# Two transformer blocks on one core: the opening's half slabs shared out anew, four attention levels with late queries only, one joint reordered

## The reference

```python
def first_block(x, ...):                     # DEPTH = 2
    for i in range(2):
        h = rms_norm(x, g[0])
        m = neighborhood_attention(h) if i == 0 else diff_attention(h)
        x = x + rms_norm(m, g[1])
        f = conv_glu_ffn(rms_norm(x, g[2]))
        x = x + rms_norm(f, g[3])
        gate = sigmoid(rms_norm(x, g[4]) @ ple_w_gate[i])
        x = x + gate * (p[i] @ ple_w_proj[i])

def second_block(h, ...):
    h = h + 0.5 * swiglu(rms_norm(h))
    o_hg = hgrn2_chunkwise(hq, log_f, k, v)  # gated linear attention, 4 heads, decay per key channel
    o_mla = causal_block_attention(q, k, v)
    h = h + concat(o_hg, o_mla) @ w_out
    h = h + 0.5 * swiglu(rms_norm(h))
    h = h + sigmoid(rms_norm(h) @ w_ple_gate) * (p @ w_ple_proj)
    return rms_norm(h)
```

## Time and profile before

| what | value |
|---|---|
| median of 3 runs | 1193.83 us (1193.71 to 1195.09) |
| the profiled execution | 1193.79 us |
| its span, first to last instruction | 1191.9 us |
| granted TensorE clock, mean | 0.998 |
| PE, PEld busy | 99%, 86% |
| DVE, ACT, POOL busy | 78%, 56%, 12% |
| weights and inputs read | 213.60 MB, 180 GB/s over the span |

### The profile page before, as it was taken

The page is one execution under the profiler, slowest core; times in us unless marked ns, Lnnn a source line. Parts: engine busy times, 40 slices in busy tenths (PEclk is TensorE's granted clock), DMA queues, the critical chain, the costliest instruction groups (busy, mean ns, idle before and its releaser), DMA issues.

```text
span 1191.9 us, 17766 instructions
## 1 busy us (share of the span) xinstructions
PE 1179.1 (99%) x6915; PEld 1028.1 (86%) x6915; DVE 933.1 (78%) x1270; ACT 665.0 (56%) x1059; POOL 139.0 (12%) x265
## 2 busy tenths in 40 slices
PE   8999999999999999999999999999999999999997
PEld 7998988888889989888888988888898888888886
DVE  6866898898777689989888898766776878766765
ACT  6756644444867786544446745444586664444445
POOL 5300600000300011000003100000206410000002
PEclk9999999999999999999999999999999999999999
DMA  9758376655544345665555575556455147556540
GB/s 297 223 156 269 124 244 207 210 179 178 190 139 148 129 163 195 212 205 185 182 173 179 184 230 189 189 187 203 136 191 177 44 161 228 176 197 204 185 142 36
DMA packets 151671, 215.83 MB, mean 181 GB/s; under 512 B 7002, under 2 KB 116956, under 8 KB 151588
## 3 DMA queue, kind: packets, MB, share of 16 engines
q1 hardware_dynamic: 148124, 207.46, 53.1%
q0 software_dynamic: 1760, 3.94, 1.3%
q10 hardware_dynamic: 1704, 3.28, 0.9%
HBM read 213.60 MB, written 1.06 MB: 180 GB/s over the span
## 4 chain that ended last, share of the span: by engine, by line
PE 93%; DVE 3%; ACT 1%; DMA 1%; issue 1%; POOL 0%; SPq 0%; POOLq 0%; ACTq 0%; DVEq 0%
PE work L2491 25%; PE work L2494 13%; PE acc L2072 10%; PE acc L2073 10%; PE acc L2074 10%; PE work L2072 5%; PE work L2073 5%; PE work L2074 5%; PE work L2094 1%; PE work L2480 1%; PE work L2468 1%; DVE w_lo L1357 1%; PE work L2482 1%; PE work L2619 1%; PE acc L2129 1%; PE acc L2270 1%
## 5 line engine op out<-in xcount | busy, mean ns | idle before, releaser
L1357 DVE TENSOR_TENSOR w_lo<-raw,w_hi 128x2048 fp32r<-128x2048 f32 (+1 forms) x192 | 436.0, 2277 | 51.5 <-ACT w_hi L752 51.5
L752 ACT ACTIVATE w_hi<-raw 128x2048 fp32r<-128x2048 f32 (+1 forms) x192 | 363.5, 1899 | 69.0 <-PE work L2494 59.4
L2491 PE MATMUL work<-hT_both,w_hi 128*128 128x512 f32 x1280 | 318.8, 391 | 0.0
L2491 PEld LDWEIGHTS work<-hT_both,w_hi 128*128 128x128 f32 x1280 | 234.8, 188 | 45.1
L2494 PEld LDWEIGHTS work<-hT_both,w_lo 128*128 128x128 f32 x1280 | 174.6, 190 | 12.5
L2494 PE MATMUL work<-hT_both,w_lo 128*128 128x256 f32 x1280 | 178.5, 282 | 0.0
L2072 PE MATMUL acc<-w_hi,aux_hi 128*128 128x512 f32 x400 | 158.0, 395 | 0.0
L2073 PE MATMUL acc<-w_lo,aux_hi 128*128 128x512 f32 x400 | 156.7, 392 | 0.0
L2074 PE MATMUL acc<-w_hi,aux_lo 128*128 128x512 f32 x400 | 155.8, 390 | 0.0
L1131 ACT ACTIVATE aux_hi<-Z 128x256 fp32r<-128x256 f32 x88 | 36.9, 419 | 195.4 <-DVE Z L1780 107.4
L1751 DVE TENSOR_REDUCE Z<-work 128x256 f32<-128x512 f32 x88 | 60.6, 689 | 89.5 <-PE work L2494 87.8
(11 more groups left out here) (283 smaller groups left out, 1740.2 us busy)
## 6 DMA issues: line engine op xcount, KB each, us to landing
raw<-in_ffn_w_in SPq DMA_DIRECT2D x44, 1024.0 KB, 5.1
raw<-in_ffn_w_out SPq DMA_DIRECT2D x22, 1024.0 KB, 5.1
raw<-in_w_gate SPq DMA_DIRECT2D x22, 1024.0 KB, 5.3
raw<-in_w_up SPq DMA_DIRECT2D x22, 1024.0 KB, 5.3
raw<-in_w_down SPq DMA_DIRECT2D x22, 1024.0 KB, 4.9
raw<-in_da_w_qkv SPq DMA_DIRECT2D x12, 1024.0 KB, 5.3
raw<-in_na_w_qkv SPq DMA_DIRECT2D x10, 1024.0 KB, 7.3
raw<-in_ple_w_gate SPq DMA_DIRECT2D x8, 1024.0 KB, 5.2
```

The lines of the kernel that those rows point to most:

```text
L752: act.activation(w_hi[:, n % RING, 0:size], raw[:, n % RAW, 0:size], ACT.Copy).then_inc(hi_done, 1)
L1357: dve.tensor_tensor(w_lo[:, n % RING, 0:size], raw[:, n % RAW, 0:size], w_hi[:, n % RING, 0:size].bitcast(F32), ALU.subtract).then_inc(lo_ ...
L2491: pe.matmul(b.rearrange("p (e s) -> p e s", e=2), v[0][:, k, cols(c % 2)], hT_both[:, k, :, :], start=k == 0, stop=False)
```

## The change

There are three parts.

1. **Opening.** ACT casts half 2 in place of half 3, ahead of the last four blocks of tile 0. POOL casts half 1, makes the second tile's root, casts half 3 and makes its low part too; DVE loses that low part. PE and SP wait on the semaphores that now belong to each half.
2. **Levels.** On levels 1 to 4 PE's moving operand is the late queries alone, 64 in place of 128, read as runs of r; the result lies packed in 64 columns for each head and tile. DVE's masked copy reads and writes 256 elements in place of 512. Level 0 and level 5 stay.
3. **Joint.** ACT and DVE take `feed(b + 6)` ahead of the sums of squares and of the scaling of tile 0; DVE adds pieces 2 and 3 before the blocks of tile 0, and piece 4 in their middle; ACT does the squares of tile 1 in three places. PE turns tile 0 in the middle of the last gate piece, behind that piece's wait, and turns tile 1 before the last step of tile 0's value rows.

```diff
@@ -370,6 +370,7 @@
         half_landed = [sem(f"half_landed{i}") for i in range(2 * FIRST)]
         act_half_hi, pool_half_hi, half_lo = sem("act_half_hi"), sem("pool_half_hi"), sem("half_lo")
+        pool_half_lo = sem("pool_half_lo")
         hi_done, lo_done = sem("hi_done"), sem("lo_done")
@@ -570,6 +571,8 @@
                 if n >= RAW:
                     sp.wait_ge(lo_done, n - RAW + 1)
+                    if n == RAW + 1:
+                        sp.wait_ge(pool_half_lo, 1)
                 if n == RELOAD:
@@ -630,10 +633,14 @@
             late_rows(pool)
             powers("pre0.0")
-            for i in (1, 2):
-                pool.wait_ge(half_landed[i], 16)
-                pool.tensor_copy(weight_half(w_hi, i), weight_half(raw, i)).then_inc(pool_half_hi, 1)
+            pool.wait_ge(half_landed[1], 16)
+            pool.tensor_copy(weight_half(w_hi, 1), weight_half(raw, 1)).then_inc(pool_half_hi, 1)
             powers("pre0.1")
+            pool.wait_ge(half_landed[3], 16)
+            pool.tensor_copy(weight_half(w_hi, 3), weight_half(raw, 3)).then_inc(pool_half_hi, 1)
+            pool.wait_ge(pool_half_hi, 2)
+            pool.tensor_tensor(weight_half(w_lo, 3), weight_half(raw, 3), weight_half(w_hi, 3).bitcast(F32),
+                               ALU.subtract).then_inc(pool_half_lo, 1)
             for i in range(32):
@@ -844,16 +851,18 @@
                 if ph == 2:
                     gates(2, 1)
+                    feed(b + 6)
                     pre(3, 0)
-                    feed(b + 6)
                     gates(2, 2)
                     gates(2, 3)
-                    tile_parts(3, 0, range(4))
+                    tile_parts(3, 0, range(2))
+                    pre(3, 1, (0,))
+                    tile_parts(3, 0, range(2, 4))
+                    pre(3, 1, (1,))
                     gates(2, 4)
                     tile_parts(3, 0, range(4, 6))
-                    pre(3, 1, (0, 1))
+                    pre(3, 1, (2,))
                     tile_parts(3, 0, range(6, 8))
-                    pre(3, 1, (2,))
                     feed(b + 7)
@@ -1293,8 +1302,8 @@
             tile_parts(0, 0, range(4))
             pre(0, 1, (1,))
+            high_half(2)
             tile_parts(0, 0, range(4, 8))
-            high_half(3)
             act.dma_start(z(11864, 12120), bass.AP(w["da_lambda"].tensor, 0, [[0, P], [1, 256]])).then_inc(lam_loaded, 16)
@@ -1494,14 +1503,13 @@
                     add_gated(2, 0)
                     add_gated(2, 1)
+                    feed(b + 6)
                     normed(3, 0)
-                    feed(b + 6)
-                    tile_parts(3, 0, range(4))
                     add_gated(2, 2)
                     add_gated(2, 3)
-                    tile_parts(3, 0, range(4, 6))
+                    tile_parts(3, 0, range(4))
                     add_gated(2, 4)
-                    tile_parts(3, 0, range(6, 8))
+                    tile_parts(3, 0, range(4, 8))
                     normed(3, 1)
@@ -1878,9 +1886,19 @@
                             continue
                         evacuated(dve, G[f"lev{i - 1}"] + q)
-                        m = lmask[:, i, :]
-                        dve.copy_predicated(A[:, 4 * q:4 * q + 4, :], bass.AP(m.tensor, m.offset, [m.ap[0], [0, 4], [1, P]]),
-                                            bank(g, 4)).then_inc(bank_free[g % WORK], 1)
+                        if i == QUAD:
+                            m = lmask[:, i, :]
+                            dve.copy_predicated(A[:, 4 * q:4 * q + 4, :],
+                                                bass.AP(m.tensor, m.offset, [m.ap[0], [0, 4], [1, P]]),
+                                                bank(g, 4)).then_inc(bank_free[g % WORK], 1)
+                            continue
+                        n, r = P // (2 * LEVELS[i]), LEVELS[i]
+                        m = lmask[:, i, r:P]
+                        to = A[:, 4 * q:4 * q + 4, r:P]
+                        dve.copy_predicated(bass.AP(to.tensor, to.offset, [to.ap[0], [P, 4], [2 * r, n], [1, r]]),
+                                            bass.AP(m.tensor, m.offset, [m.ap[0], [0, 4], [2 * r, n], [1, r]]),
+                                            bank(g)[:, 0:S].rearrange("p (a b r) -> p a b r", a=4, b=n))\
+                            .then_inc(bank_free[g % WORK], 1)
 
@@ -1981,12 +1999,12 @@
 
             def low_half(i):
-                if i in (1, 2):
-                    dve.wait_ge(pool_half_hi, i)
+                if i == 1:
+                    dve.wait_ge(pool_half_hi, 1)
                 else:
-                    dve.wait_ge(act_half_hi, 1 + i // 3)
+                    dve.wait_ge(act_half_hi, 1 + i // 2)
                 dve.tensor_tensor(weight_half(w_lo, i), weight_half(raw, i), weight_half(w_hi, i).bitcast(F32),
-                                  ALU.subtract).then_inc(lo_done if i % 2 else half_lo, 1)
+                                  ALU.subtract).then_inc(lo_done if i else half_lo, 1)
 
@@ -2022,7 +2040,6 @@
             normed(0, 1)
             low_half(2)
-            low_half(3)
             tile_parts(0, 1)
@@ -2168,14 +2185,16 @@
                             ins.then_inc(used, 1)
 
-            def value_rows(ph, half, kh, t):
+            def value_rows(ph, half, kh, t, ks=range(4)):
                 v, g = slab(B[ph] + VALUE_SLABS[ph][half] + kh), G[f"v{ph}.{half}.{t}"]
                 b = open_bank(pe, g) if kh == 0 else work[:, g % WORK, :]
-                for k in range(4):
+                for k in ks:
                     if ph == 3 and half == 0:
                         split_done(pe, ph, t, 4 * kh + k)
                     ins = product3(b, both(hT, every, 4 * kh + k, cols(t)), both(v, every, k, every),
                                    kh == 0 and k == 0, kh == 1 and k == 3)
+                if ks[-1] < 3:
+                    return
                 if kh == 1:
@@ -2208,10 +2227,12 @@
                 for j in range(2):
                     if j == 1:
-                        if ph + 1 not in UNSCALED:
+                        if ph + 1 not in UNSCALED and ph != 2:
                             turn_x(ph + 1, 0)
                         pe.wait_ge(sig_done, 5 * ple_index(ph) + 3)
                     for kh in range(2):
+                        if ph == 2 and j == 1 and kh == 1:
+                            turn_x(3, 0)
                         v = slab(n + 2 + kh)
@@ -2235,10 +2256,10 @@
                     k, half = BLOCKS[4 * kh + i], 2 * kh + i // 2
                     if t == 0 and i % 2 == 0:
-                        if half in (1, 2):
-                            pe.wait_ge(pool_half_hi, half)
+                        if half % 2:
+                            pe.wait_ge(pool_half_hi, 1 + half // 2)
                         else:
-                            pe.wait_ge(act_half_hi, 1 + half // 3)
+                            pe.wait_ge(act_half_hi, 1 + half // 2)
                     split_done(pe, 0, t, k)
@@ -2247,7 +2268,12 @@
                 for i in range(4):
                     if t == 0 and i % 2 == 0:
-                        pe.wait_ge(lo_done if i else half_lo, kh + 1)
+                        if kh == 0:
+                            pe.wait_ge(lo_done if i else half_lo, 1)
+                        elif i == 0:
+                            pe.wait_ge(lo_done, 2)
+                        else:
+                            pe.wait_ge(pool_half_lo, 1)
                     ins = pe.matmul(b, hT_hi[:, BLOCKS[4 * kh + i], cols(t)], w_lo[:, kh, cols(i, 512)],
@@ -2389,8 +2415,9 @@
             def attention3():
                 value_rows(3, 0, 0, 0)
-                value_rows(3, 0, 1, 0)
+                value_rows(3, 0, 1, 0, range(3))
                 turn_x(3, 1)
+                value_rows(3, 0, 1, 0, range(3, 4))
                 value_rows(3, 0, 0, 1)
@@ -2616,8 +2643,13 @@
                         for h in range(2):
                             for t in range(T):
-                                ins = pe.matmul(d[ks, cols(2 * h + t)][:, qs], k[:, 2 * j + h, cols(t)][:, ks],
-                                                q[:, 2 * j + h, cols(t)][:, qs], start=True, stop=True)
+                                if 0 < i < QUAD:
+                                    late = q[:, 2 * j + h, cols(t)].rearrange("p (b e r) -> p b e r", e=2, r=LEVELS[i])
+                                    ins = pe.matmul(d[:, cols(2 * h + t, 64)].rearrange("p (b r) -> p b r", r=LEVELS[i]),
+                                                    k[:, 2 * j + h, cols(t)], late[:, :, 1, :], start=True, stop=True)
+                                else:
+                                    ins = pe.matmul(d[ks, cols(2 * h + t)][:, qs], k[:, 2 * j + h, cols(t)][:, ks],
+                                                    q[:, 2 * j + h, cols(t)][:, qs], start=True, stop=True)
                         ins.then_inc(bank_full[g % WORK], 1)
```

## The result

The changed kernel takes 1196.24 us in the median of 22 runs (1194.03 to 1197.36), the kernel before 1194.13 in as many (1193.67 to 1195.11). The ratio is 1.0013 with a 95% interval of 1.0007 to 1.0019: **slower by some 2 us**, where 1192.8 was forecast and 1194.1 was the top of the range. The runs before lie within 1.5 us of each other; those after spread over 3.3, seven from 1194.0 to 1194.9 and fifteen from 1195.6 to 1197.4.

What follows compares the result with a forecast made beforehand. The prediction took TensorE (PE), holding 93% of the chain, to bound the kernel. From 1193.79 us it took 0.6 for the opening, 0.0 for the levels and 0.4 for the joint, giving 1192.8, range 1190.9 to 1194.1.

Steps and rivals of the forecast that it cites:

- the step that failed: Opening: DVE starts scaled rows near 13.7, ahead of POOL's subtraction, then goes straight to half 2's low part; gain 0.6.
- The first rival: Opening: POOL's subtraction takes the port before DVE's scaled rows; 0 to 0.25 lost, 1193.5 with the joint; chance 0.10.
- at nothing, since PE meets neither: Opening: SP's slab 4 load waiting for POOL's 17.55 and POOL's memsets ending near 18.5 were priced at nothing.
- A price: Opening: POOL's subtraction, which had no row, was priced at 1.94 from POOL's 128x1024 operation at L697.
- Levels: Levels 1 to 4: halved queries gain nothing, as 128-column weight loads keep records at 0.111.
- Joint: Joint of phases 2 and 3: block 6 met 0.3 later, yet the second tile starts at 345.63; gain 0.4.
- The root operation held: Joint: POOL's first root operation, asking at 331.1, is held by DVE's slab subtraction until 333.3; scaling at 334.35.
- Rival A: Joint: the root is not held, scaling at 333.15; gain 1.9 + 0.6, giving 1191.3; chance 0.13.

Runs made afterwards that it cites:

- scaled rows as one: The changed kernel with the second tile's scaled rows as one instruction and the memsets behind POOL's wait for the third slab's cast: 1194.02 us, ratio 1.0005.
- POOL behind DVE: The changed kernel with POOL's subtraction waiting for DVE's low part of half 2, and the memsets behind the third slab's cast: 1194.09 us, ratio 1.0001.
- the joint's slab in halves: The changed kernel with half 3's low part on DVE, the memsets moved later, and the joint's slab cast and subtraction cut in two: 1193.04 us, ratio 0.9993.
- the joint alone: The kernel before with the joint's part of the change alone: 1193.71 us, ratio 0.9996.
- again: The changed kernel once more, unaltered, for one profiled look: 1195.59 us.
- opening alone: The kernel before with the opening's part of the change alone: 1195.3 us, ratio 1.0012.
- 64 keys: The changed kernel with 64 instead of 128 weight columns on levels 1 to 4, leaving out half of the keys' results there: 1193.92 us.
- memsets late: The changed kernel with POOL's 32 memsets moved behind its wait for the third slab's cast: 1193.93 us, ratio 1.0002.

## Why the prediction was wrong

**Opening, the step that failed.** "DVE starts the scaled rows near 13.7, ahead of POOL's new subtraction, and goes straight on to half 2's low part." It did start first, at 13.91, and did not go on: POOL's subtraction got in behind the first half, and the second, 0.48 by itself, lasted 3.51 (2.60 in other executions). Where a gain of 0.6 was forecast, 2.36 were lost. I took a row of DVE instructions for one holder of the port. The run with the scaled rows as one instruction shows that a waiting POOL operation gets in where one DVE instruction ends and the next would begin: there the low part was held, 3.39 instead of 1.21. The rows that I argued from did not show that: at 319.52 one POOL operation waited for one DVE instruction, so no second DVE instruction stood behind the one that ran.

**The first rival had the right engine and the wrong price.** It had POOL ahead of all of the scaled rows, and its 0 to 0.25 counted only the low part's delay. Left out were that PE's turning waits on the second half, that the memsets stand next in POOL's list, and that PE, left standing, comes back on the lower clock. Together they made 2.36 of it. The memsets had their own row at 14.21, and that they had held DVE was read; that they would now follow the subtraction was taken as "at nothing, since PE meets neither".

**A price.** POOL's subtraction took 2.36 to 2.46 where 1.94 of another operation was used. With that and the right order (the run with POOL behind DVE) the opening gains nothing: the second tile starts 9.35 behind the cast, where the forecast had 8.59, and of the 0.76 some 0.4 is the subtraction's length and some 0.35 its later start. The root ahead of a cast and ACT's cast of half 2 may gain something when DVE keeps half 3: 0.3 to 0.4 from the cast to the second tile in two executions and 0.75 in a third (the run with the joint's slab in halves), where like openings differ by 0.4.

**Levels: right.** 0 forecast, 0.108 a record after, 0.9999 alone, and for the reason given: 64 weight columns brought 0.061.

**Joint: right, to 0.1 in each step.** The root operation held (2.18, forecast 2.2), scaling at 334.33 (334.35), block 6 at 341.17 (341.26), the second tile at 345.62 (345.63). The gain, 0.42 here and 0.46 in the joint alone, is seen in the traces; the timed runs alone (0.9996, 0.9987 to 1.0005) are too coarse for it. Rival A, a root not held, falls by the 2.18. Its price was not tested cleanly: with most of the hold gone the joint gained 0.68, not 1.9, but the second half of the subtraction then stood in the way.

## What to carry to other kernels

Here DVE gave up the port that it shares with POOL at the end of each instruction; POOL's row of 32 short instructions, which overlap one another, let DVE in nowhere. When a long operation is moved onto the second engine, look for the boundary at which it will get in, and at what stands behind that boundary on the first, not at who starts first. If the most loaded engine, here PE, is left standing for it, it may then work on a lower clock for a while, and that can cost as much as the stall or more. And look at the spread of the runs: where it grows, as here from 1.4 to 3.3 us, one profile shows only one course of several.

## What was not expected of the hardware

- **The fall of PE's clock.** In seven executions PE stood for 1.2 to 2.1 us around the turning of the second tile (14 to 19 us). Behind that the granted clock was 0.50 for some 3.4 us in four (changed, again, opening alone, 64 keys: gaps of 2.08, 2.12, 1.20 and 1.15) and stayed at 1.00 in three (memsets late, POOL behind DVE, scaled rows as one: 1.17, 1.72 and 1.79). So the gap alone does not decide, and its length does not either; what does was not found. With idle products in the gap the clock stayed too; that is one profile, borne out by eleven runs of which one is above 1195.6, where fifteen of 22 of the changed kernel were. Of the kernels whose profile shows no fall, some have a run or two near 1195.8 (memsets late 1195.92, scaled rows as one 1195.68 and 1195.76); whether it fell there is not known.
- **The memsets after the subtraction.** DVE's second half was held for 3.51 in three executions, where the memsets followed the subtraction at once and ran first, and for 2.6 in two with the same list of POOL, where DVE got in between them. Which of the two comes is not settled either. Between the 32 memsets themselves DVE got in nowhere: each lasts 0.09 to 0.10 and the next starts 0.03 behind it, so that one of them is always running. That this is why they hold DVE as one block is argued, not tested.
- **The port is exclusive for an instruction's whole length**, as the Trainium skill has it (SBUF — State Buffer, section Who interferes with whom); here a half of 0.48 lasted 2.60 under POOL's one subtraction. That POOL, waiting, is served at DVE's next boundary is this case's finding, in seven executions; that DVE is served so at POOL's boundaries it does not show.
